# Index scoring begun in the kv projection, stacking on two queues, gating group 1 first, and seven evictions in ten search rounds

## Chip, core and metric

The kernel runs on one core of one Trainium2 chip. The metric is device time in microseconds (us) of one execution, as the median of several runs. The engines are named as the profile does: PE is TensorE, DVE VectorE, ACT ScalarE, POOL GpSimd, SP SyncE.

## The reference, cut to what matters

One decoder layer on 1024 tokens of 1024 channels. The change touches the first part: the combined projection, the index scores of the sparse attention, the choice of the 256 best keys of each query, and the convolution.

```python
proj = jnp.einsum('bsd,de->bse', x, w_in[l])
q, c_kv, iq, ik, iw, u_pool, u_conv = jnp.split(proj, SPLIT_POINTS, axis=-1)
c_kv = rms_norm(c_kv, kv_norm_g[l])
...
logits = jnp.einsum('bqhd,bsd->bqhs', iq_b, ik).astype(jnp.float32)
idx_score = jnp.einsum('bqhs,bqh->bqs', jax.nn.relu(logits), iw_b.astype(jnp.float32))
idx_score = jnp.where(causal[None], idx_score, -jnp.inf)
_, sel = lax.top_k(idx_score, topk)
...
a, gate = jnp.split(u, 2, axis=-1)
h = a * jax.nn.sigmoid(gate)
h = lax.conv_general_dilated(h, conv_w, ...) + conv_b    # causal, width 31, per channel
h = layer_norm(h, ln_g, ln_b)
return jax.nn.silu(h)
```

After it come the softmax attention over the chosen keys, the output projection with a first norm, and a mixture of 16 experts (two of them for each token) with a second norm. These are the same in both kernels.

## The kernel before

Everything is written out by hand: each engine has its own block of instructions, issued in the order in which the Python loops emit them, and the engines meet at semaphores (`wait_ge`, `then_inc`). No scheduler moves anything.

**Units.** The projection is cut by columns into 14 tiles (`COLS`): index keys and weights (`ikw`), index queries `iq0` and `iq1`, `kv`, two tiles of `gate`, two of `a` (the two halves of the gated linear unit of the convolution; the number is the group of 128 channels), two of `pool`, four of `q`. A tile has two units of 512 tokens. `UNITS` lists them in order, with small units between them: the transposed index weights `iwT`, the mean square `ms` of kv, its spread `mr`. After the projections (`PROJECTIONS`) come 8 `key` and 8 `val` units. A projection unit is 24 matmuls (`three`: values are kept as a high and a low part, and three products of them are summed). Its weights go through `w_raw`, `w_hi` (a cast by ACT in `w_split`) and `w_lo` (a subtraction by DVE in `w_split`); each has two buffers, so tile j needs both parts done, and they overwrite those of tile j-2. Projection units have four PSUM banks: unit k waits until unit k-4 has been evicted, by ACT, or by DVE for `a` units, whose eviction multiplies by the sigmoid of the gate into `hpad` (the gating product).

**Index scores.** `IDX` has 48 products, one for each of six query blocks (`BLOCKS`) and eight heads. PE multiplies `stack_iq` by `stack_ik`, ACT applies relu, DVE weights and sums into `bias`, with two buffers between each pair of engines. The stacks hold the parts of the index queries and keys at other partitions than the projection leaves them, and are filled by SP with small DMAs (`stack`). `plan()` hangs six products on every projection unit from `LATER` on, and one on every small unit.

**Search.** The 256th best score of each query is found by bisection in 25 rounds (`ROUNDS`). In a round DVE counts three blocks and ACT three others (`count`), and DVE makes the next candidates from both. Units that are left over after the last index product (`rest`) are evicted in the rounds, one to a round, on DVE and on ACT; when only key and value units are left, ACT evicts two to a round. When DVE has no projection unit left, it builds in each round the diagonal matrices `diag` of `TAPS_PER_ROUND` taps: PE makes 24 taps (`TAPS_PE`) of the convolution of group 0 as matmuls with them.

**PE's order.** After the last projection unit come four key units, then one tap and one key or value unit by turns, taps up to 18, the first scores of the attention (`qk`), the taps 18 to 23, the pooling's products, and then the attention. POOL makes the other group's taps by itself, from the moment when all of DVE's unit work and all index sums are done.

Of the kernel before, what the change touches and what calls it, by code (L numbers as in the profile page):

```python
# [16 lines left out]
P = 128  # L17
# [24 lines left out]
        + [("kv", COL_KV, HALVES)]  # L42
        + [(f"gate{i}", COL_CONV + 256 + P * i, HALVES) for i in range(2)]
        + [(f"a{i}", COL_CONV + P * i, HALVES) for i in range(2)]
        + [(f"pool{i}", COL_POOL + P * i, HALVES) for i in range(2)]
# [3 lines left out]
for _j, (_n, _c, _r) in enumerate(COLS):  # L49
    UNITS += [(_n, i, _j) for i in range(len(_r))]  # L50
    if _n == "iq1":
        UNITS += [("iwT", 0, None), ("iwT", 1, None)]
    if _n == "kv":
        UNITS += [("ms", 0, None)]
    if _n == "gate0":
        UNITS += [("mr", 0, None), ("mr", 1, None)]
# [15 lines left out]
TAPS_EARLY = 18  # L72
TAPS_PER_ROUND = 4
IDX_PER_UNIT = 6
# [141 lines left out]
def program(nc, a):  # L216
    ctx = ExitStack()
    with ctx:
# [274 lines left out]
        POOL_UNITS = seen(BY_ACT, UNITS.index(("pool1", 1, [c[0] for c in COLS].index("pool1"))))  # L493
        LATER = [k for k, u in enumerate(UNITS) if u[0] == "gate0"][0]

# [7 lines left out]
        PLAN = list(plan())  # L503
        LAST_IDX = max(i for i, p in enumerate(PLAN) if len(p[1]))

        block = ctx.enter_context(nc.Block())
# [3 lines left out]
        def _(sp):  # L510
# [30 lines left out]

            def stack(i):
                for part in range(4):
                    rows = slice(part * IDIM, (part + 1) * IDIM)
                    src = iqT_hi if part < 2 else iqT_lo
                    for h4 in range(4):
                        sp.dma_start(f32(stack_iq[rows, 4 * i + h4, :]), f32(src[h4 * IDIM:(h4 + 1) * IDIM, i, :])
                                     ).then_inc(stack_in[i], 16)
# [5 lines left out]
            sp.wait_ge(unit_dve, seen(BY_DVE, UNITS.index(("iq0", 1, 1))))  # L554
            stack(0)
            w_tile(5)
            sp.wait_ge(unit_dve, seen(BY_DVE, UNITS.index(("iq1", 1, 2))))
            stack(1)
            for j in range(6, len(COLS)):
# [459 lines left out]
        def _(act):  # L1019
# [13 lines left out]
            def unit(k):  # L1033
# [27 lines left out]
                elif name[:4] == "gate":  # L1061
                    if name == "gate0" and i == 0:
                        act.wait_ge(unit_mm, UNITS.index(("iwT", 1, None)) + 1)
# [16 lines left out]
            def item(k, between):  # L1080
                _, i, j = UNITS[k]
                if j is not None and i == 0 and j + 1 < len(COLS):
                    w_split(j + 1)
                for u in between:
                    index(u)
                unit(k)

            for p in PLAN[:LAST_IDX + 1]:
                item(*p)
            rest = PLAN[LAST_IDX + 1:]  # L1090

# [12 lines left out]
            for r in range(ROUNDS):  # L1104
                count(r)
                for _ in range(1 if rest and rest[0][0] < PROJECTIONS else 2):
                    if rest:
# [220 lines left out]
        def _(dve):  # L1328
# [35 lines left out]
            def unit(k):  # L1364
# [25 lines left out]
                elif name[0] == "a":  # L1390
                    ti = int(name[1])
                    if k == UNITS.index(("a0", 0, [c[0] for c in COLS].index("a0"))):
                        dve.memset(hpad[:, :, 0:PAD_H], 0.0).then_inc(pads_set, 1)
                    dve.wait_ge(unit_mm, k + 1)
                    dve.wait_ge(unit_act, seen(BY_ACT, [q for q, u in enumerate(UNITS) if u[0] == "gate1"][1]))
                    dve.tensor_tensor(hpad[:, ti, PAD_H + t0:PAD_H + t0 + n], src, sig[:, ti, t0:t0 + n], ALU.mult
# [43 lines left out]
            for r in range(ROUNDS):  # L1440
# [8 lines left out]
                if rest:  # L1449
                    item(*rest.pop(0))  # L1450
                elif taps < TAPS_PE:
# [627 lines left out]
```

## Time and profile before

| | us |
|---|---|
| median of 3 runs | 991.65 |
| lowest, highest | 990.85, 996.98 |
| span of the profiled execution | 989.0 |
| PE busy in it | 906.2 (92%) |
| DVE, ACT, POOL busy | 687.2, 560.2, 360.3 |

The profiler took one execution; its own time outside the profiler isn't listed, only its span from the first to the last instruction. Times in the rows below count from the start of that span. A duration in the timeline runs to the modelled end of an instruction, and the next one may start before it; a row with x8 stands for eight instructions in a run. A bracket at a row's end gives the idle time of the engine ahead of it, and what ended it.

### The profile page before, as it was taken

What the parts mean: (1) busy time and instruction counts of PE and PEld (TensorE: products, weight loads), DVE (VectorE), ACT (ScalarE), POOL (GpSimd) and SP (SyncE); (2) the same over time, 40 slices, a digit from 0 to 9 for tenths busy, and PEclk for the clock granted to TensorE, in tenths of its full rate; (3) what the DMA queues carried; (4) which work ended last, traced back from release to release, by engine and by line L of the source; (5) the groups of instructions that cost most, each with busy time, mean ns of one, the idle gap of its engine ahead of it and who ended that gap; (6) DMA issues with size and microseconds to landing.
All of it is one profiled execution on the core that took longest, in us unless ns stands there. A gap on an engine that the chain in (4) does not pass through costs nothing.

```text
span 989.0 us, 15968 instructions
## 1 busy us (share of the span) xinstructions
PE 906.2 (92%) x4804; PEld 712.6 (72%) x4805; DVE 687.2 (69%) x1033; ACT 560.2 (57%) x805; POOL 360.3 (36%) x271
## 2 busy tenths in 40 slices
PE   6999999999898899999918999999999999999990
PEld 6877888744466567888807888888878888888770
DVE  5339888898789875737687747889888854234276
ACT  5256567686787665702233647777777743225342
POOL 0000079999999980000001112222332321111137
PEclk9999999999999999999959999999999999999995
DMA  8550111000000100533576879999999987552475
GB/s 234 146 139 22 43 43 65 1 0 2 1 2 1 44 1 23 169 119 130 230 286 216 268 253 317 391 403 382 404 403 382 404 282 241 177 148 45 108 243 211
DMA packets 63486, 172.54 MB, mean 174 GB/s; under 512 B 19297, under 2 KB 33633, under 8 KB 51120
## 3 DMA queue, kind: packets, MB, share of 16 engines
q1 hardware_dynamic: 55664, 143.85, 39.4%
q0 software_dynamic: 7488, 27.07, 11.0%
q10 hardware_dynamic: 288, 1.05, 0.3%
q8 instruction: 24, 0.39, 0.2%
q14 instruction: 22, 0.18, 0.1%
HBM read 142.79 MB, written 26.74 MB: 171 GB/s over the span
## 4 chain that ended last, share of the span: by engine, by line
PE 45%; DMA 9%; DVE 6%; ACT 2%; issue 2%; DVEq 0%; ACTq 0%; POOLq 0%; POOL 0%; SPq 0%
PE ps L472 13%; PE ps L474 12%; PE ps L473 12%; DMA raw<-in_w_gate 9%; PE ps L950 2%; DVE wlo L1762 1%; PE ps L824 1%; ACT whi L1248 1%; DVE sm L1608 1%; PE ps L791 1%; PE ps L986 1%; PE ps L874 1%; PE ps L811 1%; DVE xgT_lo L1772 0%; DMA xg<-x_d,slot_token 0%
## 5 line engine op out<-in xcount | busy, mean ns | idle before, releaser
L1762 DVE TENSOR_TENSOR wlo<-raw,whi 128x2048 fp32r<-128x2048 f32 x96 | 216.1, 2288 | 51.9 <-ACT whi L1248 51.8
L1248 ACT CAST whi<-raw 128x2048 fp32r<-128x2048 f32 x96 | 180.3, 1911 | 50.0 <-DMA raw<-in_w_gate 17.5
L472 PE MATMUL ps<-whi,xgT_hi 128*128 128x512 f32 x384 | 152.0, 396 | 6.7 <-DVE xgT_lo L1772 6.7
L474 PE MATMUL ps<-whi,xgT_lo 128*128 128x512 f32 x384 | 149.8, 390 | 0.0
L473 PE MATMUL ps<-wlo,xgT_hi 128*128 128x512 f32 x384 | 149.6, 390 | 0.0
L472 PEld LDWEIGHTS ps<-whi,xgT_hi 128*128 128x128 f32 x384 | 72.3, 188 | 22.9 <-issue 7.1
L472 PE MATMUL ps<-xT_hi,w_hi 128*128 128x512 f32 (+1 forms) x224 | 87.0, 388 | 1.7 <-DVE xT_lo L1360 1.7
L1986 POOL COPY idx_now<-slot_token 128x1 int32 (+1 forms) x24 | 8.0, 334 | 218.2 <-PE ps L950 218.2
L473 PE MATMUL ps<-xT_lo,w_hi 128*128 128x512 f32 (+1 forms) x224 | 85.7, 383 | 0.0
L474 PE MATMUL ps<-xT_hi,w_lo 128*128 128x512 f32 (+1 forms) x224 | 85.7, 383 | 0.0
L474 PEld LDWEIGHTS ps<-whi,xgT_lo 128*128 128x128 f32 x384 | 72.1, 188 | 15.4
L473 PEld LDWEIGHTS ps<-wlo,xgT_hi 128*128 128x128 f32 x384 | 72.2, 188 | 14.2
L472 PE MATMUL ps<-whi,hT_hi 128*128 128x512 f32 x192 | 77.5, 404 | 0.5 <-issue 0.5
L1447 DVE TENSOR_SCALAR_CACHE_REDUCE junk_dve<-bias,sm 128x1024 bf16<-128x1024 f32 (+2 forms) x75 | 75.7, 1009 | 1.8
L474 PE MATMUL ps<-whi,hT_lo 128*128 128x512 f32 x192 | 75.7, 394 | 0.0
L473 PE MATMUL ps<-wlo,hT_hi 128*128 128x512 f32 x192 | 75.6, 394 | 0.0
L2001 POOL DMA_INDIRECT acc_d<-ysb,idx_add x23 | 40.9, 1778 | 92.8 <-ACT ysb L1275 91.9
L1099 ACT ACTIVATE junk_act<-bias,sm 128x768 bf16<-128x768 f32 (+2 forms) x75 | 62.2, 829 | 16.5 <-DVE sm L1465 12.6
L1543 DVE CUSTOM_DVE_ANT_0 probs<-ps,bias 128x128 f32<-128x128 f32 (+7 forms) x64 | 45.9, 754 | 18.3 <-PE ps L791 13.8
L1265 ACT ACTIVATE silu<-ps 128x512 f32<-128x512 f32 x24 | 14.3, 594 | 76.4 <-PE ps L474 76.4
L1779 DVE SCALAR_TENSOR_TENSOR hid<-silu,slot_gate,ps 128x512 f32<-128x512 f32 x24 | 17.8, 744 | 55.4 <-ACT silu L1265 55.4
L1896 POOL TENSOR_SCALAR tapped<-hpad,par 128x512 f32<-128x512 f32 x32 | 56.0, 1759 | 0.1
(333 smaller groups left out, 1923.9 us busy)
## 6 DMA issues: line engine op xcount, KB each, us to landing
raw<-in_w_gate SPq DMA_DIRECT2D x32, 1024.0 KB
raw<-in_w_up SPq DMA_DIRECT2D x32, 1024.0 KB
raw<-in_w_down SPq DMA_DIRECT2D x32, 1024.0 KB
w_raw<-in_w_in SPq DMA_DIRECT2D x14, 512.0 KB, 4.0
x_tok<-in_x SPq DMA_DIRECT2D x8, 512.0 KB, 7.8
wo_raw<-in_w_o SPq DMA_DIRECT2D x16, 256.0 KB, 2.8
x_res<-in_x SPq DMA_DIRECT2D x16, 256.0 KB, 3.4
x_d<-xa SPq DMA_DIRECT2D x4, 512.0 KB, 6.0
```

The lines of the kernel that those rows point to most:

```text
L472: pe.matmul(out, l_hi, r_hi, start=start, stop=False)
L473: pe.matmul(out, l_hi, r_lo, start=False, stop=False)
L474: return pe.matmul(out, l_lo, r_hi, start=False, stop=stop)
L950: last = pe.transpose(pair(2)[:, k * P:(k + 1) * P], xg[:, k::KT], ident[:])
L1099: act.activation(junk_act[:, 0:WIDTH[b]], bias[:, AT[b]:AT[b] + WIDTH[b]], ACT.Sign, bias=cands[r % 2][:, c:c + 1], scale=-1.0, accum_out= ...
L1248: act.copy(whi[:, n, :], raw[:, n, :]).then_inc(gu_hi if n < 4 else dn_hi, 1)
L1447: dve.tensor_scalar(junk_dve[:, 0:WIDTH[b]], bias[:, AT[b]:AT[b] + WIDTH[b]], now[:, c:c + 1], 0.0, ALU.is_lt, ALU.add, accum_out=res[:, c ...
L1543: dve.tensor_tensor_reduce(out=probs_at(u)[:, 0:WIDTH[b]], in0=scores_at(u, WIDTH[b]), in1=bias[:, AT[b]:AT[b] + WIDTH[b]], scale=-1.0, sc ...
L1762: dve.tensor_tensor(wlo[:, n, :], raw[:, n, :], f32(whi[:, n, :]), ALU.subtract).then_inc(gu_lo if n < 4 else dn_lo, 1)
L1779: dve.scalar_tensor_tensor(hid[:], silu[:], slot_gate[:, bass.ds(t, 1)], ps[:, 1, :], ALU.mult, ALU.mult).then_inc(hid_set, 1)
L1896: pool.tensor_scalar(tapped[:, half], src[:, half], by, None, ALU.mult).then_inc(tap_mul, 1)
L2001: pool.indirect_dma_start(acc_d, bass.IndirectOffsetOnAxis(ap=idx_add[:], axis=0), ysb[:], None, compute_op=ALU.add).then_inc(y_out, 16)
```

## The change

- `COLS` puts group 1 of the gated unit first: `gate1`, `a1`, `gate0`, `a0` instead of `gate0`, `gate1`, `a0`, `a1`. The `mr` units stand behind `gate1`, an `a` unit waits only for the gate of its own group, and the padding of `hpad` is cleared at `a1`.
- `LATER` is the first `kv` unit instead of the first unit of `gate0`, so index products start three units earlier. The last one stands in the second unit of `gate0`; 14 projection units instead of 12 are left for the rounds.
- `stack(0)` on SP keeps the high parts; the eight copies of the low parts are issued by ACT behind the first unit of `iq1`.
- ACT casts the high part of tile j+2 behind the second unit of tile j, and no longer ahead of the index products of tile j+1's first unit. DVE's subtraction stays where it was.
- `in_round(r)` gives seven projection units to ten rounds, on DVE and ACT: rounds 1, 2, 4, 5, 7, 8, 9, 11, 12, 14, 15, 17, 18, 19. Diagonals come after them, six taps to a round instead of four.

```diff
         + [("kv", COL_KV, HALVES)]
-        + [(f"gate{i}", COL_CONV + 256 + P * i, HALVES) for i in range(2)]
-        + [(f"a{i}", COL_CONV + P * i, HALVES) for i in range(2)]
+        + [(f"{n}{i}", COL_CONV + c + P * i, HALVES) for i in (1, 0) for n, c in (("gate", 256), ("a", 0))]
...
-    if _n == "gate0":
+    if _n == "gate1":
         UNITS += [("mr", 0, None), ("mr", 1, None)]
...
-TAPS_PER_ROUND = 4
+TAPS_PER_ROUND = 6
...
-        LATER = [k for k, u in enumerate(UNITS) if u[0] == "gate0"][0]
+        LATER = [k for k, u in enumerate(UNITS) if u[0] == "kv"][0]
...
+        def in_round(r):
+
+            return (r + 1) * 7 // 10 - r * 7 // 10
...
-            stack(0)
+            stack(0, range(2))
             w_tile(5)
             sp.wait_ge(unit_dve, seen(BY_DVE, UNITS.index(("iq1", 1, 2))))
-            stack(1)
+            stack(1, range(4))
...
             def item(k, between):
                 _, i, j = UNITS[k]
-                if j is not None and i == 0 and j + 1 < len(COLS):
-                    w_split(j + 1)
+                if j == 0 and i == 0:
+                    w_split(1)
                 for u in between:
                     index(u)
                 unit(k)
+                if j is not None and i == 1 and j + 2 < len(COLS):
+                    w_split(j + 2)
 
             for p in PLAN[:LAST_IDX + 1]:
                 item(*p)
+                if UNITS[p[0]][:2] == ("iq1", 0):
+                    act.wait_ge(unit_dve, seen(BY_DVE, UNITS.index(("iq0", 1, 1))))
+                    for part in range(2, 4):
+                        for h4 in range(4):
+                            act.dma_start(f32(stack_iq[part * IDIM:(part + 1) * IDIM, h4, :]),
+                                          f32(iqT_lo[h4 * IDIM:(h4 + 1) * IDIM, 0, :])).then_inc(stack_in[0], 16)
...
             for r in range(ROUNDS):
                 count(r)
-                for _ in range(1 if rest and rest[0][0] < PROJECTIONS else 2):
+                for _ in range(in_round(r) if rest and rest[0][0] < PROJECTIONS else 2):
                     if rest:
                         item(*rest.pop(0))
...
                 if rest:
-                    item(*rest.pop(0))
+                    for _ in range(in_round(r)):
+                        item(*rest.pop(0))
                 elif taps < TAPS_PE:
```

On PE, in the first kv unit: the rows are its matmuls (lines L472 to L474 before, L471 to L473 after), from the same place of the program on. Before:

```order
L472 MATMUL ps<-xT_hi,w_hi 128x512
L473 MATMUL ps<-xT_lo,w_hi 128x512
L474 MATMUL ps<-xT_hi,w_lo 128x512
L472 MATMUL ps<-xT_hi,w_hi 128x512
L473 MATMUL ps<-xT_lo,w_hi 128x512
L474 MATMUL ps<-xT_hi,w_lo 128x512
```

After:

```order
L471 MATMUL ps<-xT_hi,w_hi 128x512
L472 MATMUL ps<-xT_lo,w_hi 128x512
L473 MATMUL ps<-xT_hi,w_lo 128x512
L719 MATMUL ps<-stack_ik,stack_iq 128x512 x2
L471 MATMUL ps<-xT_hi,w_hi 128x512
L472 MATMUL ps<-xT_lo,w_hi 128x512
```

The index products (`stack_ik`, `stack_iq`), which came first in the first unit of `gate0`, now stand between the matmuls of `kv`.

On ACT, at the start of the search: `junk_act` rows are the three counts of a round, `w_hi` a cast, `uT` the eviction of a pool unit. Before:

```order
L1099 ACTIVATE junk_act,sm<-bias,sm 128x768
L1099 ACTIVATE junk_act,sm<-bias,sm 128x640
L1099 ACTIVATE junk_act,sm<-bias,sm 128x512
L1024 CAST w_hi<-w_raw 128x1024
L1069 COPY uT<-ps 128x512
L1099 ACTIVATE junk_act,sm<-bias,sm 128x768
L1099 ACTIVATE junk_act,sm<-bias,sm 128x640
L1099 ACTIVATE junk_act,sm<-bias,sm 128x512
L1069 COPY uT<-ps 128x512
```

After:

```order
L1027 CAST w_hi<-w_raw 128x1024
L1110 ACTIVATE junk_act,sm<-bias,sm 128x768
L1110 ACTIVATE junk_act,sm<-bias,sm 128x640
L1110 ACTIVATE junk_act,sm<-bias,sm 128x512
L1110 ACTIVATE junk_act,sm<-bias,sm 128x768
L1110 ACTIVATE junk_act,sm<-bias,sm 128x640
L1110 ACTIVATE junk_act,sm<-bias,sm 128x512
L1110 ACTIVATE junk_act,sm<-bias,sm 128x768
L1110 ACTIVATE junk_act,sm<-bias,sm 128x640
L1110 ACTIVATE junk_act,sm<-bias,sm 128x512
L1027 CAST w_hi<-w_raw 128x1024
```

Every round had an eviction; now rounds 0 to 2 have none on ACT (DVE evicts the `a0` units in rounds 1 and 2), and the cast stands ahead of the search and at the end of round 2.

On DVE, where the first diagonals are built: three counts, the diagonals, and the step to the next candidates. Before, in round 12 of 25:

```order
L1442 TENSOR_SCALAR ps<-ps 128x6
L1447 TENSOR_SCALAR junk_dve,sm<-bias,sm 128x1024
L1447 TENSOR_SCALAR junk_dve,sm<-bias,sm 128x896
L1447 TENSOR_SCALAR junk_dve,sm<-bias,sm 128x384
L1455 TENSOR_TENSOR diag<-ps,par 128x512
L1462 TENSOR_TENSOR sm<-sm,ps 128x6
```

After, in round 20:

```order
L1453 TENSOR_SCALAR ps<-ps 128x6
L1458 TENSOR_SCALAR junk_dve,sm<-bias,sm 128x1024
L1458 TENSOR_SCALAR junk_dve,sm<-bias,sm 128x896
L1458 TENSOR_SCALAR junk_dve,sm<-bias,sm 128x384
L1467 TENSOR_TENSOR diag<-ps,par 128x768
L1474 TENSOR_TENSOR sm<-sm,ps 128x6
```

The diagonals move from rounds 12 to 17 to rounds 20 to 23, and each of the four instructions makes six taps (768 columns) instead of four (512).

## Rows read from the trace of the kernel before

**Rows 1.** Waits of PE from 38 to 246 us: total, times, longest

```profile
PE ps L716 <- ACT relu L1078: 2.2, 3, 1.4
PE ps L680 <- ACT sq L1042: 0.8, 1, 0.8
```

**Rows 2.** Busy time of each engine in two stretches, PE's clock behind POOL

```profile
128.00:193.80 65.80, 65.80 (x285) 53.13 (x283) 56.52 (x133) 47.02 (x96) 62.48 (x31) 1.00 0.13 41
193.80:246.00 52.20, 52.20 (x126) 22.99 (x125) 48.20 (x136) 40.81 (x89) 49.46 (x21) 1.00 0.01 1
```

**Rows 3.** Timeline of PE: start, us, line, operation

```profile
46.44 0.48 PE L472 MATMUL ps<-xT_hi,w_hi 128*128 128x512 f32 x1
...
124.89 0.33 PE L716 MATMUL ps<-stack_ik,stack_iq 128*128 128x384 f32 x1
...
179.71 0.39 PE L473 MATMUL ps<-xT_lo,w_hi 128*128 128x512 f32 x1
179.94 0.39 PE L474 MATMUL ps<-xT_hi,w_lo 128*128 128x512 f32 x1
...
190.37 3.59 PE L691 MATMUL ps<-cT,wuk 128*128 128x512 f32 x8
193.80 1.88 PE L745 MATMUL ps<-hpad,diag 128*128 128x512 f32 x4
...
245.97 1.02 PE L839 MATMUL ps<-sums,wpool 128*128 128x512 f32 x2
```

**Rows 4.** Timeline of DVE in the search

```profile
126.91 0.68 DVE L1396 TENSOR_TENSOR hpad<-ps,sig 128x512 f32<-128x512 f32 x1
...
128.00 0.17 DVE L1442 TENSOR_SCALAR ps<-ps 128x6 f32<-128x6 f32 x1
...
133.59 0.17 DVE L1442 TENSOR_SCALAR ps<-ps 128x6 f32<-128x6 f32 x1
...
137.43 0.17 DVE L1442 TENSOR_SCALAR ps<-ps 128x6 f32<-128x6 f32 x1
...
192.26 0.68 DVE L1455 TENSOR_TENSOR diag<-ps,par 128x512 f32<-128x512 f32 x1
...
243.88 0.16 DVE L1467 SCALAR_TENSOR_TENSOR sm<-sm,ps 128x6 f32<-128x6 f32 x1
```

**Rows 5.** Busy time of DVE for w_lo alone, in the search

```profile
128.00:190.00 62.00, 9.70 (x5) 1.00 0.14 43
```

**Rows 6.** The tile w_lo: durations in ns, least, median, most

```profile
L1353 DVE TENSOR_TENSOR w_lo<-w_raw,w_hi x14: 1204/1226/2858, 6.0 to 173.2; 128x1024 fp32r<-128x1024 f32 x14
```

**Rows 7.** Timeline of ACT: square, table load, three relus

```profile
57.62 0.60 ACT L1042 ACTIVATE sq<-ps 128x512 f32<-128x512 f32 x1 [4.36 <-PE ps L474]
...
58.71 1.28 ACT L1054 ACT_TABLE_LOAD   x1
...
62.27 3.31 ACT L1078 ACTIVATE relu<-ps 128x1024 f32<-128x1024 f32 x3 [0.75 <-PE ps L716]
```

**Rows 8.** Timeline of SP's queue: issues of stack copies

```profile
38.84 4.95 SPq L547 DMA_DIRECT2D stack_iq<-iqT_hi  x8
43.84 6.20 SPq L547 DMA_DIRECT2D stack_iq<-iqT_lo  x8
```

**Rows 9.** Timeline of ACT at iq1's second unit

```profile
45.85 0.58 ACT L1052 CAST iqT_hi<-ps 128x512 fp32r<-128x512 f32 x1 [5.10 <-PE ps L474]
```

**Rows 10.** Timeline of POOL: its first taps, its last sum

```profile
127.78 1.19 POOL L1886 TENSOR_SCALAR conv<-hpad,par 128x1024 f32<-128x1024 f32 x1 [0.35 <-DVE hpad L1396]
129.13 2.86 POOL L1889 TENSOR_SCALAR tapped<-hpad,par 128x1024 f32<-128x1024 f32 x1 [0.17 <-POOL conv L1886]
...
364.64 2.51 POOL L1944 TENSOR_TENSOR conv<-conv,extra 128x512 f32<-128x512 f32 x2 [2.54 <-DVE extra L1520]
```

**Rows 11.** The chain that ended last, at the convolution's mean

```profile
369.58 2.58 PE ps L845 x6
```

**Rows 12.** Busy time and PE's clock after the output projection

```profile
497.00:500.00 3.00, 0.00 (x0) 0.00 (x0) 2.76 (x11) 3.00 (x2) 0.00 (x0) 0.50 1.02 431
```

More of the change, by code:

```diff
@@ L540, in _, with stack @@
                 w_tile(j)
-            def stack(i):
-                for part in range(4):
+            def stack(i, parts):
+                for part in parts:
                     rows = slice(part * IDIM, (part + 1) * IDIM)
@@ L1061, in unit @@
                 elif name[:4] == "gate":
-                    if name == "gate0" and i == 0:
+                    if name == "gate1" and i == 0:
                         act.wait_ge(unit_mm, UNITS.index(("iwT", 1, None)) + 1)
@@ L1391, in unit @@
                     ti = int(name[1])
-                    if k == UNITS.index(("a0", 0, [c[0] for c in COLS].index("a0"))):
+                    if k == UNITS.index(("a1", 0, [c[0] for c in COLS].index("a1"))):
                         dve.memset(hpad[:, :, 0:PAD_H], 0.0).then_inc(pads_set, 1)
                     dve.wait_ge(unit_mm, k + 1)
-                    dve.wait_ge(unit_act, seen(BY_ACT, [q for q, u in enumerate(UNITS) if u[0] == "gate1"][1]))
+                    dve.wait_ge(unit_act, seen(BY_ACT, [q for q, u in enumerate(UNITS) if u[0] == f"gate{ti}"][1]))
                     dve.tensor_tensor(hpad[:, ti, PAD_H + t0:PAD_H + t0 + n], src, sig[:, ti, t0:t0 + n], ALU.mult
```

## Prediction

> **What bounds the kernel now.** I read the waits of TensorE first, since the page shows it 92% busy: from 38 to 246 us it waits three times for a relu eviction (2.2 us in all) and once for a square (0.8 us), and for nothing else [rows 1]. Then the stretches: TensorE has no idle time from 128.0 to 193.8 us and none from 193.8 to 246.0 us [rows 2]. So the whole stretch from the first projection to the last convolution tap is set by TensorE's own fixed order of instructions. Its timeline says what is in it [rows 3]: the last projection matmuls run up to 190.37 us, 0.23 us apart (24 to a unit: 5.47 us); four key units; the first tap at 193.80 us; then one tap and one key or value unit by turns, and the last taps alone, up to 245.97 us. The convolution needs 52.2 us from its first tap. The search of VectorE and ScalarE ends at 243.88 us [rows 4], about 2 us ahead of TensorE. The two are balanced, but the attention starts behind TensorE's last tap.
>
> **How the search is paced.** A round of the search without anything else takes 3.84 us (133.59 to 137.43 us) [rows 4]. A round in which VectorE also splits weights is longer by the split: five splits were busy for 9.7 us in the search [rows 5], and one of them takes from 1.20 to 2.86 us [rows 6]. TensorE doesn't mind any of it: it gets one eviction in every round, its units take 5.47 us, and the rounds follow it.
>
> **Index scoring begun earlier.** 13 index products go into the kv units and the mean-square unit, so the last one stands in the second unit of gate0 rather than of a1. Between the first kv matmul (46.44 us) and the last index product (124.89 us) [rows 3] lie 78.4 us; two plain units less (10.9 us) puts it at 114.0 us with the same waits. The waits change. The relu of the eleventh product and the square after it now stand ahead of the mean-square unit: a relu takes 1.0 us (three in 3.31 us) and the square 0.6 us [rows 7], which with their starts some tenths late gives TensorE about 1.7 us of wait there, 0.8 us before [rows 1]. The table loads for square root and sigmoid (1.28 us each) [rows 7] fall between relus: about 1.9 us against the 2.2 us of now. Stacked queries of group 1 come about 0.8 us late (next part). Together 4.4 us against 3.0 us. I take 1.1 us of it; bounds are minus 3.0 us (no wait at all) and plus 3. From the last index product to the first round were 3.1 us, 0.7 us of them a gating product [rows 4] that now comes later: the search starts at 114.0 + 2.4 + 1.1 = 117.5 us, 10.5 us earlier than the 128.00 us of now.
>
> **Stacking on two queues.** SyncE issues eight copies in 5.0 us and eight more in 6.2 us [rows 8]. ScalarE stands idle for 5.1 us before its eviction at 45.85 us [rows 9], and its eight issues, at the same 0.62 us each, just fit. The first stack is then in place at about 48 us, when TensorE reaches the first index product (46.44 + 1.4 = 47.8 us). The second stack starts when its source is ready (45.85 + 0.58 us for the eviction and some 0.7 us for VectorE's part: 47.1 us), and takes 16 issues, 10 us; with an estimated 2 us to land it is there at about 59.2 us, 0.8 us after its product could run. If an issue costs ScalarE twice as much, the eviction at 45.85 us is 5 us late and up to 3 us reach TensorE; that lies inside the bound above.
>
> **Seven evictions in ten rounds.** This decides the case. Fourteen projection units are left for the rounds, and in_round spreads them over rounds 1 to 19. VectorE builds the diagonals of the taps only when none is left, in rounds 20 to 23 (six taps each). TensorE's order is unchanged: first tap behind the fourth key. Round 20 starts at 117.5 + 20 x 3.84 = 194.3 us, plus what VectorE does besides in these rounds: one split before GpSimd is at work (1.1 us, the median of 1.23 us less the overlap of 0.1 us with its neighbours), five beside it at the mean of now (9.7 us busy, 9.2 us of added time), two gating products (1.2 us), and two late counts of ScalarE behind a w_hi cast (0.6 us): 206.4 us. The counts take 3.1 us, the diagonals of four taps took 0.68 us [rows 4], of six about 0.95 us: the first tap can start at 210.5 us, and started at 193.80 us. TensorE itself would be there earlier, but not by as much as in the kernel before: a unit's weights are split in the round of the unit two before it, so TensorE also waits 2 to 3 us at pool 1, q0 and q3 and ends its projections at about 201 us; with four keys (3.4 us) it stands at the tap from about 205 us. These waits run beside the search and cost nothing of their own. Behind the first tap nothing holds it: six taps to a round are more than it uses, keys are evicted two to a round from round 20 on. So the last tap ends at 210.5 + 52.2 = 262.7 us against 245.97 us: **16.7 us later**.
>
> **What is not gained.** The search itself ends at 206.4 + 4 x 4.7 + 3.84 = 229 us, 15 us earlier than now. Nothing uses this: VectorE's next work is the masked maximum of the first scores, which TensorE makes behind tap 18. GpSimd starts its own taps when the last gating product is done; that is in round 2, at about 131 us, against 127.78 us [rows 10]. It ended at 367.1 us, and the mean of the convolution was taken at 369.58 us [rows 10, 11]; with attention some 17 us later these 3 us are covered. If the cover were gone they would cost at most 3 us. The attention itself may lose some crowding with GpSimd, under 1 us; I take nothing.
>
> **The clock.** After TensorE stood still from 494 us on, its granted clock was 0.50, the 1.2 GHz level [rows 12]. The new wait of about 5.5 us ahead of the first tap may end in the same: if the first 3 us behind it run at the low level, they cost about 1.5 us. From nothing to 3 us; I take 1.
>
> **The sum.** 16.7 + 1.0 = 17.7 us. The profiled execution has a span of 989.0 us; its own time isn't given apart from it, and the median of the three runs, 991.65 us, is 2.65 us over that span. I put the sum on the median: **1009 us**.
>
> **Rivals.**
> Faster, because the search sets the start of attention: TensorE's order would have to have slack, and the 15 us by which the search ends earlier would come through: 977 us. For it: the search ended only 2 us ahead of the last tap, a difference that a small edit could turn. Against it: no idle time in 52.2 us of taps [rows 2], and an order that puts all taps ahead of the second scores. It decides if round 20 starts before 189.7 us, since then the tap isn't held; that is 17 us short. 8%.
> About the same: every bound at its low end. Splits that GpSimd doesn't stretch (1.1 us each, 3.6 us less), no new wait in the index products (3 us less), a clock that holds: 10 us are left, 1001.6 us. The median split of 1.23 us stands for it, the five of the search with their mean of 1.94 us [rows 5, 6] against it. 14%.
> The splits are stretched more: each waits for the GpSimd operation that is under way. A GpSimd product lasts 2.86 us [rows 10], and so did the longest split [rows 6]; at that length for all five it is 4.3 us more, with a late clock 1016 us. The Trainium skill (SBUF — State Buffer, section Who interferes with whom) calls the port pair that VectorE and GpSimd share an exclusive lock, held for a whole instruction. The spread from 1.20 to 2.86 us agrees with it. By that rule a split could at worst wait out a whole product, 1.2 + 2.9 us, and five of them take 20 us instead of 9.7; that end would be 1019 us, an estimate from the same rows. 8%.
> The change doesn't spread the work as it says: the order shows it does; I give this nothing.
>
> **Chances.** A measurement of this kernel can tell about 1% (9.9 us) from no change. The forecast with its bounds has 70%, of which all but the low end is slower by over 1%; with the stretched splits that makes slower 0.78, same 0.14, faster 0.08. The range reaches from the low bounds (10 us less one or two) to the high ones (16.7 + 4.3 + 3 for the clock and index waits together, 24 us): 1000 to 1016 us. Only the search-bound case lies far outside.
>
> **What would show it.** In the profile after: rounds begin at 116 to 120 us; the search ends near 229 us; TensorE waits for w_lo two or three times between 136 and 190 us, and 4 to 8 us for diag ahead of its first tap, which starts near 210 us; the last tap ends near 263 us, and from there to the end it takes as long as from 246 us now. Wrong would be: a first tap before 203 us, rounds shorter than 3.84 us, or an attention that is shorter by more than 3 us.

## Result and profile after

The changed kernel takes **1012.51 us** (median of 4 runs, 1011.13 to 1013.59), the kernel before 992.2 us in the runs beside it. The ratio is 1.0189, 95% interval 1.016 to 1.0218: slower by nearly 2%. The forecast was 1009 us with a range of 1000 to 1016 us, and slower by over 1% with a chance of 0.78. The span of the profiled execution is 1011.2 us, 22.2 us longer than before. Executions of one and the same kernel differ by up to 1%, and with their mean granted clock: on the chip of the last run below, the kernel before took from 990.3 us (clock 0.970) to 1000.7 us (0.960), so a difference of a few us in one trace can be one of clock alone.

The waits of PE from 38 to 270 us in the changed kernel (total, times, longest) answer to [rows 1], where nothing but three relus and a square stood:

```profile
PE ps L471 <- DVE w_lo L1364: 7.1, 3, 3.1
PE ps L748 <- DVE diag L1467: 3.6, 1, 3.6
PE ps L719 <- DMA stack_iq<-iqT_lo: 2.3, 1, 2.3
PE ps L683 <- ACT sq L1045: 1.9, 1, 1.9
PE ps L694 <- ACT qT L1074: 1.5, 1, 1.5
PE ps L842 <- ACT conv L1162: 0.3, 1, 0.3
PE ps L719 <- ACT relu L1081: 0.3, 1, 0.3
```

Five kinds of wait are new or longer: for the low half of the weights, for the diagonals, for the stacked queries, for the square, and for the eviction of a q unit ahead of the fourth key. PE's timeline (start, duration) answers to [rows 3]:

```profile
50.22 0.72 PE L719 MATMUL ps<-stack_ik,stack_iq 128*128 128x512 f32 x2 [2.34 <-DMA stack_iq<-iqT_lo]
...
118.01 0.33 PE L719 MATMUL ps<-stack_ik,stack_iq 128*128 128x384 f32 x1
...
204.03 2.74 PE L694 MATMUL ps<-cT,wuk 128*128 128x512 f32 x6
208.24 1.13 PE L694 MATMUL ps<-cT,wuk 128*128 128x512 f32 x2 [1.48 <-ACT qT L1074]
212.94 3.75 PE L748 MATMUL ps<-hpad,diag 128*128 128x512 f32 x4 [3.58 <-DVE diag L1467]
...
268.02 1.02 PE L842 MATMUL ps<-sums,wpool 128*128 128x512 f32 x2
```

The last index product starts 6.9 us earlier than before (118.01 against 124.89 us), but the keys start 13.7 us later, the first tap 19.1 us later, and the last tap ends 22.05 us later (268.02 against 245.97 us). From there to the end of the span it takes 743.2 us, and took 743.0 us. So the whole loss is made before the last tap.

DVE's timeline, to be read beside [rows 4], shows the first round, round 20 with the diagonals in it, and the end of the search:

```profile
120.66 0.17 DVE L1453 TENSOR_SCALAR ps<-ps 128x6 f32<-128x6 f32 x1
...
208.73 0.17 DVE L1453 TENSOR_SCALAR ps<-ps 128x6 f32<-128x6 f32 x1
...
211.85 0.95 DVE L1467 TENSOR_TENSOR diag<-ps,par 128x768 f32<-128x768 f32 x1
...
230.47 0.16 DVE L1479 SCALAR_TENSOR_TENSOR sm<-sm,ps 128x6 f32<-128x6 f32 x1
```

The search ends 13.4 us earlier than before, and nobody gains by it. Windows of the changed kernel (busy time of each engine; the number after POOL's count is PE's granted clock, full speed being 1.00) around the first index product and around the first tap:

```profile
50.00:52.00 2.00, 1.78 (x7) 1.41 (x8) 0.00 (x0) 1.02 (x1) 0.00 (x0) 0.85 0.62 151
52.00:54.00 2.00, 2.00 (x6) 1.62 (x5) 1.06 (x2) 1.03 (x2) 0.00 (x0) 0.50 0.66 161
54.00:56.00 2.00, 2.00 (x8) 1.61 (x8) 1.15 (x2) 1.03 (x1) 0.00 (x0) 0.80 0.65 157
211.00:214.00 3.00, 1.06 (x2) 0.57 (x3) 2.86 (x10) 2.22 (x5) 2.84 (x2) 0.64 0.01 3
214.00:217.00 3.00, 3.00 (x5) 1.27 (x4) 2.93 (x7) 2.94 (x8) 2.85 (x2) 0.50 0.00 0
217.00:220.00 3.00, 3.00 (x6) 1.25 (x5) 2.86 (x8) 2.16 (x6) 2.83 (x2) 0.72 0.00 0
```

Behind both waits the clock falls to 0.50, the 1.2 GHz level, for some microseconds. From first tap to last it takes 55.1 us instead of the 52.2 us of before [rows 2, 3], so the fall at the tap costs 2.9 us.

### The profile page after: what moved, and what is told of

It reads as the page before. It is cut to its first block, busy times and chain, and to the rows that moved or that the text cites. A ratio compares the mean times of both kernels' runs of the same rounds, so it can differ in the third digit from the quotient of the medians.

```text
span 1011.2 us, 15966 instructions
## 1 busy us (share of the span) xinstructions
PE 914.2 (90%) x4804; PEld 716.5 (71%) x4805; DVE 686.1 (68%) x1031; ACT 560.1 (55%) x805; POOL 355.4 (35%) x271
## 4 chain that ended last, share of the span: by engine, by line
PE 43%; DMA 9%; DVE 6%; issue 3%; ACT 2%; DVEq 0%; ACTq 0%; POOLq 0%; SPq 0%; POOL 0%
PE ps L471 12%; PE ps L473 12%; PE ps L472 12%; DMA raw<-in_w_gate 8%; DVE wlo L1774 2%; PE ps L953 2%; PE ps L827 1%; ACT whi L1259 1%; DVE sm L1620 1%; PE ps L794 1%; PE ps L877 1%; PE ps L989 1%; PE ps L814 1%; DVE xgT_lo L1784 0%; DMA xg<-x_d,slot_token 0%
## 5 line engine op out<-in xcount | busy, mean ns | idle before, releaser
L471 PE MATMUL ps<-whi,xgT_hi 128*128 128x512 f32 x384 | 152.0, 396 | 6.5 <-DVE xgT_lo L1784 6.5
L473 PE MATMUL ps<-whi,xgT_lo 128*128 128x512 f32 x384 | 149.8, 390 | 0.0
L472 PE MATMUL ps<-wlo,xgT_hi 128*128 128x512 f32 x384 | 149.5, 389 | 0.0
L471 PE MATMUL ps<-xT_hi,w_hi 128*128 128x512 f32 (+1 forms) x224 | 88.4, 395 | 9.0 <-DVE w_lo L1364 7.1
L471 PEld LDWEIGHTS ps<-whi,xgT_hi 128*128 128x128 f32 x384 | 72.3, 188 | 22.6 <-issue 6.9
L473 PE MATMUL ps<-xT_hi,w_lo 128*128 128x512 f32 (+1 forms) x224 | 87.3, 390 | 0.0
L472 PE MATMUL ps<-xT_lo,w_hi 128*128 128x512 f32 (+1 forms) x224 | 87.1, 389 | 0.0
L473 PEld LDWEIGHTS ps<-whi,xgT_lo 128*128 128x128 f32 x384 | 72.1, 188 | 15.3
L472 PEld LDWEIGHTS ps<-wlo,xgT_hi 128*128 128x128 f32 x384 | 72.2, 188 | 14.2
L471 PE MATMUL ps<-whi,hT_hi 128*128 128x512 f32 x192 | 77.6, 404 | 0.5 <-issue 0.5
L1458 DVE TENSOR_SCALAR_CACHE_REDUCE junk_dve<-bias,sm 128x1024 bf16<-128x1024 f32 (+2 forms) x75 | 75.7, 1009 | 1.8
L473 PE MATMUL ps<-whi,hT_lo 128*128 128x512 f32 x192 | 75.6, 394 | 0.0
L472 PE MATMUL ps<-wlo,hT_hi 128*128 128x512 f32 x192 | 75.6, 394 | 0.0
L471 PEld LDWEIGHTS ps<-xT_hi,w_hi 128*128 128x128 f32 x224 | 43.0, 192 | 19.3 <-issue 8.5
```

The lines of the kernel that those rows point to most:

```text
L471: pe.matmul(out, l_hi, r_hi, start=start, stop=False)
L472: pe.matmul(out, l_hi, r_lo, start=False, stop=False)
L473: return pe.matmul(out, l_lo, r_hi, start=False, stop=stop)
L1458: dve.tensor_scalar(junk_dve[:, 0:WIDTH[b]], bias[:, AT[b]:AT[b] + WIDTH[b]], now[:, c:c + 1], 0.0, ALU.is_lt, ALU.add, accum_out=res[:, c ...
```

## Experiments

The theory is that of the prediction: the count of rounds that the evictions are spread over sets when the diagonals are made, these set the first tap, and the rest follows it, within the few us that the clock adds or takes. Rivals are the new waits by themselves, the clock, and the split of the stack copies. Twelve kernels were run. Times are given as the ratio to the kernel before on the same chip, with the 95% interval. Events are from each kernel's own trace.

**One eviction a round** (the changed kernel, all else kept).

```diff
-            return (r + 1) * 7 // 10 - r * 7 // 10
+            return 1
```

> The changed kernel with one projection eviction in every round again (in_round returns 1); all else as changed. Theory R (the rate of evictions holds TensorE back, by late weight splits and late diagonals): TensorE ends gate0 at about 118 us, 14 units of 5.47 us and four keys bring it to its first tap at about 199 us, against 212.9 us with seven in ten and 193.8 us before; time 996 to 999 us. Rival Q (the early index scoring costs it: waits for the stack and the square, and the low clock behind them): most of the 20 us stay, 1008 us or more.

Measured: 999.29 us, 1.0068 (1.0048 to 1.0087). Rounds begin at 120.50 us as in the changed kernel, but the diagonals are made in round 14 at 196.12 us, and the last tap ends at 249.82 us, 18.2 us earlier. The waits for w_lo and diag are gone, and the time is at the upper end of what the theory gave. The rate alone is 12 to 13 of the 20 us. What is left to 992 us is the start, and an attention of 136.4 us instead of 133.3 us (last tap to first matmul of the output projection).

**The rate alone, in the kernel before** (seven in ten on ACT and DVE, six taps to a round; the order of units, the gate and the stacks stay).

```diff
-TAPS_PER_ROUND = 4
+TAPS_PER_ROUND = 6
...
-                for _ in range(1 if rest and rest[0][0] < PROJECTIONS else 2):
+                for _ in range(in_round(r) if rest and rest[0][0] < PROJECTIONS else 2):
```

> The kernel before with only the new rate: seven evictions in ten rounds and six taps to a round. Theory R: twelve units need rounds 1 to 17, diagonals come in round 18, which begins at about 128 + 18 x 3.84 + 10 for splits + 3 for waits on the high halves, 210 us; first tap at about 214 us, time 1009 to 1013 us. Rival Q: 992 to 995 us.

Measured: 1013.45 us, 1.021 (1.0169 to 1.0252). The rate alone makes all of the slowdown; what the other parts of the change are worth beside it can't be told from nothing: by the two intervals they may win up to some 7 us or lose up to some 3 us. The time is just above the 1009 to 1013 us of the theory. The waits of PE in this kernel:

```profile
PE ps L472 <- DVE w_lo L1357: 5.7, 3, 4.2
PE ps L695 <- ACT qT L1075: 5.4, 1, 5.4
PE ps L749 <- DVE diag L1460: 2.6, 1, 2.6
```

The first tap starts at 211.78 us and the last ends at 265.82 us, though the rounds begin at 127.74 us, 7.1 us later than in the changed kernel.

**All stack copies on SP.**

```diff
-            stack(0, range(2))
+            stack(0, range(4))
...
-                if UNITS[p[0]][:2] == ("iq1", 0):
-                    act.wait_ge(unit_dve, seen(BY_DVE, UNITS.index(("iq0", 1, 1))))
-                    for part in range(2, 4):
...
```

> The changed kernel with all stack copies issued by SyncE. If issue time is what limits the stack, the first stack is in place 2 us later (52 us for 50.2) and the second about 4 us later, TensorE's waits in the kv units grow by 3 to 5 us, and the rounds begin and the time ends later by as much: 1015 to 1018 us. If the copies are limited by the DMA engines that both queues share, no change: 1011 to 1013 us.

Measured: 1014.7 us, 1.0233 (1.0189 to 1.0277), which cannot be told from the changed kernel. The 3 to 5 us that were expected, if issue time is the limit, are a miss: PE waits 3.3 us for the stack instead of 2.3 us. Two of the runs below (four more matmuls, nine in ten), whose stack code is that of the changed kernel, waited 3.2 and 3.4 us. So the second queue gives at most about 1 us, and not even that is shown.

**Scoring begun at gate1** (index products from the first gate unit on, all else as changed).

```diff
-        LATER = [k for k, u in enumerate(UNITS) if u[0] == "kv"][0]
+        LATER = [k for k, u in enumerate(UNITS) if u[0] == "gate1"][0]
```

> The changed kernel with index scoring begun at the first gating unit again (LATER), so twelve units are left for the rounds, at seven in ten. Theory R: rounds begin at about 128 us, diagonals come in round 18 at about 207 us, first tap at about 211 us: 1009 to 1012 us, so the early scoring by itself is worth nothing at this rate. Rival Q: the waits in the kv units are gone, 1000 us or less.

Measured: 1016.53 us, 1.0242 (1.0197 to 1.0286). Rounds begin at 129.32 us, 8.7 us later than in the changed kernel, yet the first tap starts at 212.15 us, 0.8 us earlier. Two fewer units are left for the rounds, so the diagonals come in round 18 instead of 20: what early scoring wins at the start of the search, it gives back in rounds. The time is 4 us longer than that of the changed kernel, which was not expected, and their intervals overlap. The trace puts nothing of it ahead of the last tap, which ends 1.0 us earlier (267.01 us); all is behind it, where the clock was lower (0.96 against 0.99 in the attention).

**Four more matmuls ahead of the wait for the diagonals** (they write a bank that isn't in use; the output stays as it was).

```diff
+                if w == 0:
+                    for _ in range(4):
+                        pe.matmul(ps[:, 6, :], wuk[:, 0:2, :]..., cT[:, 0:512], start=True, stop=True)
                 pe.wait_ge(diag_set, w // TAPS_PER_ROUND + 1)
```

> The changed kernel with four matmuls more on TensorE ahead of its wait for the first diagonals (their product is overwritten later and used by nothing; 0.86 us each). Theory: the clock fell in the wait, and the low level behind it made the taps last 55.1 us for 52.2. Kept busy, TensorE keeps its clock: the first tap starts when it did (212.9 us), the taps take 52.2 to 52.5 us, time 1009 to 1010 us. Rival (the low clock has another cause, or the four matmuls only move the start): 1012 to 1014 us.

Measured: 1013.9 us, 1.0205 (1.018 to 1.0229). The windows around the first tap, the third number from the end again without PE standing still:

```profile
211.00:214.00 3.00, 2.94 (x7) 1.06 (x6) 2.86 (x9) 2.19 (x7) 2.84 (x2) 1.00 0.01 3
214.00:217.00 3.00, 3.00 (x8) 1.33 (x7) 2.93 (x6) 2.94 (x7) 2.85 (x2) 1.00 0.00 0
217.00:220.00 3.00, 3.00 (x8) 1.32 (x7) 2.86 (x10) 2.19 (x5) 2.83 (x2) 1.00 0.00 0
```

Half of the expectation held: the clock stays at 1.00, the taps take 52.3 us, and the last one ends at 265.82 us although the first starts 0.6 us later than in the changed kernel. The other half didn't: the 2.2 us won at the last tap are not in the time. The first output projection is 0.8 us ahead (400.92 against 401.74 us), and 1.6 us are lost behind it. The 1.4 us lost in the attention go with a clock of 0.97 in it, against 0.99. All this is within the scatter of the runs, so a gain of 2 us in the time is neither shown nor excluded.

**The low half split earlier on DVE** (behind the second unit of tile j, as ACT does with the high half).

```diff
-                if j is not None and i == 0 and j + 1 < len(COLS):
-                    w_split(j + 1)
+                if j == 0 and i == 0:
+                    w_split(1)
...
                 unit(k)
+                if j is not None and i == 1 and j + 2 < len(COLS):
+                    w_split(j + 2)
```

> The changed kernel with VectorE's subtraction for tile j+2 right behind the second unit of tile j, as ScalarE's cast already is. TensorE then waits less for w_lo (7.1 us in three waits now). Theory: those waits run beside the search and are covered, since the diagonals come in round 20 whatever TensorE does; they turn into a longer wait ahead of the first tap, and the time stays at 1011 to 1014 us. Rival (the late splits are part of the cost): 1005 to 1008 us.

Measured: 1020.36 us, 1.0269 (1.0241 to 1.0297), slower than the changed kernel, and a miss of the theory and of the rival both. Its timeline of DVE shows one part of it:

```profile
160.80 2.90 DVE L1364 TENSOR_TENSOR w_lo<-w_raw,w_hi 128x1024 fp32r<-128x1024 f32 x1 [1.08 <-ACT w_hi L1027]
```

The waits of PE in it, from 38 to 285 us:

```profile
PE ps L471 <- DVE w_lo L1364: 7.9, 3, 3.5
PE ps L694 <- ACT qT L1074: 5.1, 2, 2.7
```

ACT makes the high half at the end of the same round (159.72 us for 1.05 us), so DVE stands 1.1 us in the round, four times over. The diagonals come at 214.89 us, 3.0 us later. PE's waits for w_lo are no shorter (7.9 against 7.1 us) and that for qT, which holds its keys, is longer (5.1 against 1.5 us). The attention is 139.0 us, 5.3 us longer. Its work is the same, but PE is busy with it for 124.8 us instead of 118.7 us, at a mean clock of 0.94 instead of 0.99; the window of the changed kernel first, then of this one:

```profile
268.02:401.74 133.72, 118.70 (x1017) 78.23 (x1016) 107.26 (x199) 96.77 (x242) 101.09 (x70) 0.99 0.03 11
270.28:409.32 139.04, 124.78 (x1018) 81.53 (x1016) 109.26 (x199) 96.44 (x242) 98.85 (x68) 0.94 0.03 11
```

**A smooth start, one eviction a round** (the load of w_tile(5) behind the second stack, ms behind gate1 and mr behind a1, so that neither stands in the way of kv).

```diff
             stack(0, range(2))
-            w_tile(5)
             sp.wait_ge(unit_dve, seen(BY_DVE, UNITS.index(("iq1", 1, 2))))
             stack(1, range(4))
+            w_tile(5)
...
-    if _n == "kv":
+    if _n == "gate1":
         UNITS += [("ms", 0, None)]
-    if _n == "gate1":
+    if _n == "a1":
         UNITS += [("mr", 0, None), ("mr", 1, None)]
```

> One eviction in every round (as the first experiment), and the three waits of the kv units taken away: the load of weight tile 5 goes behind the stack copies, and the mean-square unit stands behind gate1, the spread units behind a1. If these waits (2.3 us for the stack, 1.9 us for the square, about 1.5 us of low clock behind them) are what is left against the kernel before, 4 to 6 us less than 999.3 us: 993 to 996 us. Rival (what is left comes from the attention, which is more crowded): 998 us or more.

Measured: 993.35 us, 1.0002 (0.9983 to 1.0021). The stack wait falls from 2.3 to 0.7 us and the square wait goes; the clock is 1.00 from 46 to 56 us, and rounds begin at 116.08 us. The first tap starts at 193.23 us, where the kernel before starts it at 193.80 us. So rate and start together explain the 20 us, as expected (993 to 996 us).

**The same with 22 taps on PE and 7 on DVE**, DVE's made after the search.

```diff
-TAPS_PE = 24
-TAPS_DVE = 5
+TAPS_PE = 22
+TAPS_DVE = 7
...
```

> The same as the smooth start, and two of TensorE's 24 taps go to VectorE, which makes all its seven taps in the idle time behind the search instead of late in the attention. If TensorE's serial work up to the last tap sets the start of the attention, 3.4 us less than the smooth start, and some less for VectorE in the attention: 988 to 992 us, which would beat the kernel before. Rival (VectorE's taps, stretched by GpSimd, reach past TensorE's last tap and delay the masked maxima): no gain or slower, 994 us or more.

Measured: 992.61 us, 0.9991 (0.9975 to 1.0007): no gain that can be told. The last tap ends at 241.56 us, 3.8 us earlier, but the output projection starts at 381.61 us, 0.5 us later than without. PE now waits 4.5 us once for DVE at the start of the attention, where its waits for DVE were 2.1 us, and the mean clock in the attention is 0.94 instead of 0.96. So the gain at the last tap is lost to a longer wait on DVE and to the clock.

**Nine and eight evictions in ten rounds.** The only line changed, for nine:

```diff
-            return (r + 1) * 7 // 10 - r * 7 // 10
+            return (r + 1) * 9 // 10 - r * 9 // 10
```

> The changed kernel with nine projection steps in ten search rounds instead of seven. Theory: the rounds set when the last projection bank is free, and each further round costs its own 3.84 us. The changed kernel needs 20 rounds and starts its first tap at 212.9; with one step a round (14 rounds, the run before) it starts at 197.7. Nine in ten needs 16 rounds, so the diagonals come 4 rounds, 15.4 us, earlier than in the changed kernel: 211.8 - 15.4 = 196.4, which is where TensorE's own work ends, so first tap at 198 to 199.5, and the time is 999 to 1002. Rival: the time follows the share of rounds with a step in a line from 999.3 (all rounds) to 1012.5 (seven in ten), which gives 1003 to 1005.

> The changed kernel with eight projection steps in ten search rounds. Theory as for nine in ten: 18 rounds are needed, two fewer than in the changed kernel, so the diagonals come at 211.8 - 7.7 = 204.1 and the first tap at 205 to 206, the time is 1012.5 - 7.7 = 1004 to 1006. Rival, what makes the slowdown is the 2 to 3 us waits for the low halves and the clock that falls after the last wait, and not the count of rounds: then eight in ten, with still a wait or two, gives 1008 to 1012.

Measured: nine 996.71 us, 1.0015 (0.9991 to 1.0039); eight 1007.07 us, 1.0117 (1.0073 to 1.0161). On this chip the kernel before took 995.36 us, 3 us more than on the others, so ratios are to be compared. Both first taps come where the theory puts them (198 to 199.5 and 205 to 206 us forecast, 199.16 and 203.51 us measured, the second 1.5 us early, as are its rounds, which begin at 119.15 us). The times fit less well: that of nine is below the forecast 999 to 1002 us, and that of eight lies between what the theory and the rival gave.

**The smooth start with seven, and with nine, in ten.**

> The kernel of the smooth start (the waits in the kv projection and before the square are gone, rounds begin near 116.1 instead of 120.7) but with the seven steps in ten rounds of the changed kernel. Theory: at this rate the rounds set the first tap, so it moves with their beginning: 120.66 - 116.1 = 4.6 us earlier than in the changed kernel, first tap at 208 to 209, time 1007 to 1009. Rival: TensorE has more waits behind the low halves instead, the first tap stays at 211 or later and the time at 1011 to 1013.

> The smooth start (no waits of 2 us in the kv projection) with nine projection steps in ten search rounds. Theory: rounds begin at 115.8 as in the other runs of the smooth start, round 16 ends 75.6 us later as in the run of nine in ten, diagonals at 191.4, which is inside TensorE's own work, so first tap at 193 to 194 and end of the taps near 245.5, as with one step a round; the search ends near 223 instead of 236, so VectorE has choosing done sooner and the attention is 133.2 us as with nine in ten and not 135.7; first output projection near 379, time 0.996 to 0.999 of before. Rival: from the end of the taps the attention is set by TensorE and ScalarE and does not see when the search ended: ratio 1.000 to 1.002, as the smooth start with one step a round gave. A second rival, that work moved earlier lowers the time by the 7 us by which the rounds begin earlier than in the kernel before: 0.992.

Measured: seven 1007.87 us, 1.0138 (1.0099 to 1.0177); nine 993.01 us, 0.9983 (0.9961 to 1.0005). The last is the best of all by its median ratio, but its interval takes in 1. With nine in ten the attention is 133.1 us, and 135.7 us with one a round. I expected that because the search ends sooner, but this can't be the reason: the kernel before has its search end at 243.88 us and an attention of 133.3 us. What goes with the length in all fourteen traces is the granted clock: 133.1 to 133.8 us at a mean clock of 0.99, 134.4 to 137.9 us at 0.97 to 0.95, 139.0 and 140.1 us at 0.94. Why the clock falls more in one of them than in another stays open; each kernel has only one trace, so it may be a matter of the execution and not of the kernel.

The runs side by side, in us from each trace:

| kernel | rounds begin | round of the first diagonals | diagonals | first tap | last tap ends | ratio |
|---|---|---|---|---|---|---|
| before | 128.00 | 12 | 192.26 | 193.80 | 245.97 | 1 |
| changed, 7 in 10 | 120.66 | 20 | 211.85 | 212.94 | 268.02 | 1.0189 |
| 8 in 10 | 119.15 | 18 | 202.41 | 203.51 | 255.75 | 1.0117 |
| 9 in 10 | 122.00 | 16 | 197.62 | 199.16 | 251.33 | 1.0015 |
| one a round | 120.50 | 14 | 196.12 | 197.65 | 249.82 | 1.0068 |
| before with 7 in 10 | 127.74 | 18 | 210.68 | 211.78 | 265.82 | 1.021 |
| scoring from gate1, 7 in 10 | 129.32 | 18 | 211.05 | 212.15 | 267.01 | 1.0242 |
| smooth start, 7 in 10 | 115.83 | 20 | 207.02 | 208.12 | 262.06 | 1.0138 |
| smooth start, 9 in 10 | 115.57 | 16 | 191.20 | 192.74 | 244.91 | 0.9983 |
| smooth start, one a round | 116.08 | 14 | 191.69 | 193.23 | 245.39 | 1.0002 |

From the begin of the rounds to the diagonals there are 91.2 us with seven in ten, whether the rounds begin at 120.66 or at 115.83 us; 83.3 us with eight and 75.6 us with nine. Each round less is 3.8 to 4.0 us, about the length of a round (3.84 us). Then it stops: with one a round it is still 75.6 us with two rounds fewer, because there PE sets the rounds and not the rounds PE. In the runs of 7 or 8 in 10 PE waits 2.6 to 3.6 us for the diagonals; in the runs of 9 in 10 and of one a round not at all. That speaks for the theory against the rival of the new waits: with eight in ten there are still waits for w_lo (3.3 us), and the first tap is where the round count puts it.

What the diagonals cost by themselves is less than it seems. With one a round PE came to its first tap at 197.65 us without standing; with seven in ten it stood there from 209.4 us on, 11.7 us later, after waits of 7.1 us for w_lo and 1.5 us for a bank, which the same rounds dole out. Only the last 3.6 us are the wait for the diagonals. A kernel that made them earlier and kept the rate was not run; by these rows it could win no more than those 3.6 us and the clock behind them.

## Why the prediction was right

**The mechanism.** "VectorE builds the diagonals of the taps only when none is left" held in every run, and the rate alone, put into the kernel before, gave the whole result. Some of the signs that were named came out just beside their bounds: the rounds begin at 120.66 us (116 to 120), the wait for the diagonals is 3.6 us (4 to 8), the last tap ends at 268.0 us (near 263).

**The start, mis-sized by 3.2 us.** 117.5 us was forecast and 120.66 us measured. The last index product stands at 118.01 us and was forecast at 115.1 us. The waits ahead of it are not the reason: 2.3 us for the stack, 1.9 us for the square and 0.3 us for relu make 4.5 us, and 4.4 us were forecast. That the sum fits is luck, since its terms were 0.8, 1.7 and 1.9 us. Of it the forecast counted 1.1 us as new, and 1.5 us are. The stack wait also fell on the first stack and not, as I had it, on the second: the last of ACT's eight copies is issued at 44.7 us and the slowest copy lands 5.5 us after issue, when I reckoned with about 2 us. What was missing is the clock, a term that I had only for the tap. It fell twice ahead of the last index product, behind the stack wait (the windows from 50 to 56 us above) and again some 3 us behind the wait for the square, which ended at 68.81 us:

```profile
70.00:72.00 2.00, 2.00 (x13) 1.82 (x13) 1.09 (x1) 0.81 (x2) 0.29 (x1) 0.97 0.00 0
72.00:74.00 2.00, 2.00 (x6) 1.61 (x6) 1.34 (x3) 1.80 (x4) 0.00 (x0) 0.50 0.00 0
74.00:76.00 2.00, 2.00 (x8) 1.58 (x7) 2.00 (x3) 1.14 (x2) 0.00 (x0) 0.68 0.00 0
```

In the run with eight in ten the waits are the same, but the first of these falls is missing, and the last index product stands at 116.51 us, 1.5 us earlier. So a fall here costs about 1.5 us. The run of the smooth start, with 2.5 us of waits and neither fall, took all of it back: 4.6 us.

**Rounds 0 to 20.** 88.9 us were forecast and 88.07 us measured (120.66 to 208.73 us). Six splits were busy for 11.47 us; five of them beside GpSimd were put at 9.7 us, and the first at 1.23 us (measured 10.25 and 1.22 us). The window of w_lo alone on DVE in the changed kernel, to set beside [rows 5]:

```profile
120.00:205.00 85.00, 11.47 (x6) 0.98 0.13 38
```

The rival of splits that are stretched more (1016 us) did not come in, though the longest, 2.94 us, is as long as that rival wanted each to be.

**First tap and last tap.** From round 20 to the first tap: 4.1 us forecast, 4.2 us measured. PE stood there from 209.4 us on, not from 205 us: the keys start at 204.03 us instead of some 201 us, and the fourth key waits 1.5 us for a bank, since the q unit in it is evicted in round 19. I had missed that wait; it is hidden behind the diagonals. The last tap is 22.05 us later and was forecast 16.7 us later plus 1 for the clock. Of the 4.35 us between, 3.2 us came from the start, 1.9 us from the clock (2.9 us instead of 1), less 0.8 us in the rounds. Of the 2.9 us of clock the forecast had a third; its [rows 12] show 0.50 from 497 to 500 us, while PE was still busy for 1.36 us between 494 and 497 us, so the fall came sooner after its last work than the text has it. In the time 3.5 us are seen (1012.51 against 1009 us), or 2.6 us by the difference to the kernel before (20.3 against 17.7 us).

**"These waits run beside the search and cost nothing of their own"** held: the 7.1 us for w_lo stand in front of a further wait of 3.6 us for the diagonals. They come from the same rate, though, and with the 1.5 us for the bank they would hold the first tap if the diagonals did not; the margin is 3.6 us. The run of the smooth start with seven in ten had more of them (8.6 us) and came out 5 us faster.

**What is not gained.** The search ended at 230.5 us (229 us forecast) with no gain. GpSimd began its taps at 133.94 us (131 us forecast), ended 22.5 us later than before, and its last sum waited 22.7 us for DVE:

```profile
133.94 1.20 POOL L1898 TENSOR_SCALAR conv<-hpad,par 128x1024 f32<-128x1024 f32 x1 [13.39 <-DVE hpad L1407]
...
387.16 2.54 POOL L1956 TENSOR_TENSOR conv<-conv,extra 128x512 f32<-128x512 f32 x2 [22.65 <-DVE extra L1532]
```

So its later start is covered, as said. The rival that the search sets the start of the attention falls: a search that ends 13.4 us earlier goes with an attention that starts 22 us later.

## What to carry to other kernels

Where work that one engine must finish is doled out in the rounds of a loop on another, count the rounds until the last piece, times the length of a round, and compare that with the time at which the first engine would get there by itself; here 16 rounds fit, and 18 put the diagonals 7.7 us later. Starting the loop earlier is worth nothing if that leaves more pieces for it: two more units were two more rounds, about what the earlier start had won. When an engine's order is without gaps over a stretch, nothing that its neighbours do earlier can shorten it. A gap that a change opens there costs its length, unless a later wait covers it, and some gaps cost the clock behind them too.

## What was unexpected on the chip

**The clock behind a short wait.** A wait of 2.3 us for the stack and one of 3.6 us, with one of 1.5 us shortly ahead of it, were followed by some 5 us in which the granted clock was down to 0.50, against 1.00 when four matmuls filled the gap. But the length of a wait does not tell. Two waits for w_lo in the changed kernel are equally long:

```profile
143.22 0.47 PE L471 MATMUL ps<-xT_hi,w_hi 128*128 128x512 f32 x1 [3.06 <-DVE w_lo L1364]
...
193.02 0.47 PE L471 MATMUL ps<-xT_hi,w_hi 128*128 128x512 f32 x1 [3.08 <-DVE w_lo L1364]
```

Behind the first the clock fell to 0.50, behind the second it stayed at 1.00:

```profile
144.00:146.00 2.00, 2.00 (x6) 1.57 (x5) 1.96 (x3) 1.94 (x5) 2.00 (x1) 0.50 0.87 232
...
194.00:196.00 2.00, 2.00 (x10) 1.63 (x9) 1.93 (x5) 1.94 (x5) 1.92 (x2) 1.00 0.00 0
```

And with eight in ten neither the stack wait of 2.3 us nor the wait of 3.2 us for the diagonals was followed by a fall: the clock is 1.00 from 44 to 58 us and from 197 to 221 us, and the taps take 52.2 us. Why one wait is followed by a fall and another isn't, no run here shows.

**VectorE and GpSimd take turns, both ways.** In the changed kernel, DVE's timeline shows one of the longest splits:

```profile
175.85 2.78 DVE L1364 TENSOR_TENSOR w_lo<-w_raw,w_hi 128x1024 fp32r<-128x1024 f32 x1
```

GpSimd's timeline at the same time:

```profile
175.63 1.92 POOL L1926 TENSOR_TENSOR doubled<-uT 128x1039 f32<-128x1039 f32 x1
177.63 1.08 POOL L1932 TENSOR_TENSOR doubled<-doubled,par 64x16 f32<-64x16 f32 x1
178.80 2.85 POOL L1933 TENSOR_SCALAR doubled<-doubled,par 64x1024 f32<-64x1024 f32 x1
```

The split ends at 178.63 us, 1.08 us after the end of GpSimd's first operation (177.55 us), which is about its length when alone (1.22 us less the overlap with its neighbour). GpSimd's next one, of 16 columns, lasts 1.08 us, where the same operation lasts 0.22 us elsewhere. The Trainium skill (SBUF — State Buffer, section Who interferes with whom) calls the ports that the two share an exclusive lock, and says that a VectorE instruction with two inputs in SBUF contends with a GpSimd instruction that reads SBUF. These rows agree. The splits at 163.07 and 189.94 us, which also started inside a GpSimd tensor-tensor operation, ended 1.09 us after its end as well. But two other splits started inside a GpSimd tensor-scalar operation, which reads SBUF too: the one at 154.38 us (GpSimd's from 152.01 to 154.86 us) lasted 1.22 us, and the one at 141.22 us (140.88 to 143.73 us) 1.85 us, ending inside it. Beside that kind the rule does not show here. So a split costs from 1.2 to 2.9 us, by what GpSimd is at.

**Small copies on two queues.** Eight copies of 96 KB each took ACT 5.13 us to issue (from 40.20 us on) and SP 5.01 us (from 38.66 us on), so the issuing does run side by side. But they landed up to 5.5 us after issue, with a load of 512 KB issued between them on SP at 43.72 us; when that load came later, in the smooth start, the most was 3.9 us and PE waited 0.7 instead of 2.3 us. In all seven kernels with the stack code of the changed kernel the most was 5.3 to 6.5 us, and in the four with the smooth start 3.2 to 3.9 us. ACT's issues in its timeline (changed kernel):

```profile
40.20 5.13 ACTq L1099 DMA_DIRECT2D stack_iq<-iqT_lo  x8
```

And the tile stack_iq, all of its copies:

```profile
DMA to landing us min/median/max: 2.1/2.3/5.5
```
